# Rotary embedding in a fused decoder trunk: the swap of 32-row halves by ScalarE copies instead of DMAs inside the chip

## The reference

```python
def _rope(t, positions):
    ...
    t1, t2 = tf[..., : d // 2], tf[..., d // 2:]
    out = jnp.concatenate([t1 * cos - t2 * sin, t2 * cos + t1 * sin], axis=-1)

def _diff_attention_mixer(proj_tok, positions, lam_params, subln_g, layer_idx):
    q, k, v = jnp.split(proj_tok, 3, axis=-1)
    q = _rope(q.reshape(b, s, DIFF_HEADS, 2, DIFF_HEAD_DIM), positions)
    k = _rope(k.reshape(b, s, DIFF_HEADS, 2, DIFF_HEAD_DIM), positions)
    ...
    o = _diff_attention(q, k, v, lam)
    o = _rms_norm(o, subln_g) * (1.0 - lambda_init)
```

## Time and profile before

| | us |
|---|---|
| median of 3 runs | 978.41 |
| the three runs | 976.68, 978.41, 983.6 |
| profiled execution, first to last instruction (span) | 976.1 |
| PE busy | 951.2 |
| DVE busy | 636.7 |
| ACT busy | 469.7 |

### The profile page before, as it was taken

One profiled execution on the slowest core, in us unless ns is written; L12 is line 12 of the kernel. 1 busy time (PEld: TensorE's weight loads), 2 busy tenths in 40 slices (PEclk: granted clock), 3 DMA queues, 4 the chain that ended last, 5 costly groups with the idle time before them and its releaser, 6 DMA issues.

```text
span 976.1 us, 14093 instructions
## 1 busy us (share of the span) xinstructions
PE 951.2 (97%) x5161; PEld 819.9 (84%) x5161; DVE 636.7 (65%) x894; ACT 469.7 (48%) x708; POOL 1.2 (0%) x9
## 2 busy tenths in 40 slices
PE   6999999999999999999999999999999999999995
PEld 5788888888888888888888888888888888888884
DVE  5776656666666666655685465467877878777555
ACT  5756544444444443444464455446445364454441
POOL 0000000000000000000000000000000000000000
PEclk9999999999999999999999999999999999999998
DMA  9665465566666555656567645565565555746552
GB/s 317 222 230 182 136 210 173 184 203 193 194 191 191 186 186 192 210 186 202 166 230 202 189 141 195 169 204 158 176 190 152 177 167 155 198 151 203 198 177 86
DMA packets 149689, 182.30 MB, mean 187 GB/s; under 512 B 8016, under 2 KB 118928, under 8 KB 148880
## 3 DMA queue, kind: packets, MB, share of 16 engines
q1 hardware_dynamic: 148704, 177.25, 57.7%
q10 hardware_dynamic: 944, 4.49, 1.3%
HBM read 176.48 MB, written 2.10 MB: 183 GB/s over the span
## 4 chain that ended last, share of the span: by engine, by line
PE 71%; DVE 14%; DMA 5%; issue 4%; ACT 3%; SPq 2%; DVEq 0%; ACTq 0%
PE psum L340 27%; PE psum L341 13%; PE psum L369 9%; PE psum L368 9%; PE psum L367 9%; DVE lo_ring L794 5%; DMA layer_area<-layer_area 5%; SPq L277 2%; ACT layer_area L758 2%; PE psum L384 1%; DVE layer_area L801 1%; ACT hi_ring L588 1%; DVE psum L1088 1%; DVE layer_area L1065 1%; DVE columns L1092 1%
## 5 line engine op out<-in xcount | busy, mean ns | idle before, releaser
L340 PE MATMUL psum<-hT_split,hi_ring 128*128 128x512 f32 x1600 | 560.1, 396 | 0.0
L794 DVE TENSOR_TENSOR lo_ring<-raw_ring,hi_ring 128x1024 fp32r<-128x1024 f32 x320 | 386.3, 1223 | 240.5 <-ACT hi_ring L588 237.6
L588 ACT ACTIVATE hi_ring<-raw_ring 128x1024 fp32r<-128x1024 f32 x320 | 337.5, 1062 | 403.4 <-PE psum L341 262.1
L341 PE MATMUL psum<-hT_split,lo_ring 128*128 128x256 f32 x1600 | 445.3, 278 | 0.0
L340 PEld LDWEIGHTS psum<-hT_split,hi_ring 128*128 128x128 f32 x1600 | 300.6, 188 | 68.3
L341 PEld LDWEIGHTS psum<-hT_split,lo_ring 128*128 128x128 f32 x1600 | 301.3, 188 | 0.3
L367 PE MATMUL psum<-hi_ring,branchT_split 128*128 128x512 f32 x256 | 100.0, 391 | 0.0
L369 PE MATMUL psum<-hi_ring,branchT_split 128*128 128x512 f32 x256 | 99.7, 390 | 0.0
L368 PE MATMUL psum<-lo_ring,branchT_split 128*128 128x512 f32 x256 | 99.7, 390 | 0.0
L368 PEld LDWEIGHTS psum<-lo_ring,branchT_split 128*128 128x128 f32 x256 | 48.1, 188 | 10.0
L367 PEld LDWEIGHTS psum<-hi_ring,branchT_split 128*128 128x128 f32 x256 | 48.1, 188 | 9.9
(11 more groups left out here) (159 smaller groups left out, 650.7 us busy)
## 6 DMA issues: line engine op xcount, KB each, us to landing
raw_ring<-in_w_in_dram SPq DMA_DIRECT2D x224, 512.0 KB, 4.4
raw_ring<-in_w_out_dram SPq DMA_DIRECT2D x64, 512.0 KB, 4.8
raw_ring<-in_w_kv_mem_dram SPq DMA_DIRECT2D x32, 512.0 KB, 5.3
layer_area<-layer_area SPq DMA_DIRECT2D x48, 64.0 KB, 4.0
stage_area<-in_mem_dram SPq DMA_DIRECT2D x4, 512.0 KB, 7.5
x_residual<-in_x_dram SPq DMA_DIRECT2D x1, 2048.0 KB, 10.9
x_residual<-in_x_dram ACTq DMA_DIRECT2D x1, 2048.0 KB, 8.6
layer_area<-in_post_norm_dram ACTq DMA_DIRECT2D x2, 1024.0 KB, 6.2
```

The costliest lines, as they stand in the source:

```text
L340: mm(o, hi[:, k, P * c:P * (c + 1)], X[:, kt, :], start=kt == 0, stop=False)
L341: last = mm(o[:, SEQ:], lo[:, k, P * c:P * (c + 1)], X[:, kt, 0:SEQ], start=False, stop=kt == KT - 1)
L588: run(whi[:, slot, :], raw[:, slot, :], ACT.Copy).then_inc(hi_ready, 1)
L794: V_.tensor_tensor(wlo[:, slot, :], raw[:, slot, :], whi[:, slot, :].bitcast(f32), SUB)\
```

## The change

The four DMAs per swap become four ScalarE copies (`ACT.Copy`) of 32 x 512 numbers each, from one group of 32 partitions to its neighbour. The wait for the combine moves with them to ACT: it stands right behind `take_small` of the queries' group and of the keys' group. The semaphore `rot_loaded`, counted by 16, becomes `rot_copied`, counted by 1. SyncE's queue keeps the weights' loads alone, in the same order. DVE's program is the same but for the semaphore.

```diff
         with sp.Fori(0, PAIRS) as p:
             for g, col in enumerate((0, TOK_WIDTH, GATE_COL)):
                 column_group(p * (3 * B_UNITS) + (U_PAIR + B_UNITS * g), w_in[1], p * BCOLS + col)
-                if g == 0 and not first:
-                    swap_halves(p * 3 + (G_PAIR - 2), kT, krot)
-            swap_halves(p * 3 + G_PAIR, qT, qrot)
...
+        def swap_halves(G, src, dst):
+
+            act.wait_ge(bank_free, G + 1)
+            for b in range(4):
+                o = 32 * (b ^ 1)
+                run(dst[32 * b:32 * b + 32, :], src[o:o + 32, :], ACT.Copy).then_inc(rot_copied, 1)
+
         def pair(p, s, first=False):
             G, u = p * 3 + G_PAIR, p * (3 * B_UNITS) + U_PAIR
             column_group(G, u, s, at={} if first else {2: lambda: exps(p - 1)})
+            swap_halves(G, qT, qrot)
             column_group(G + 1, u + B_UNITS, 1 - s,
                          at={} if first else {2: lambda: take_weights(p - 1), 3: lambda: take_values(p - 1)})
+            swap_halves(G + 1, kT, krot)
             column_group(G + 2, u + 2 * B_UNITS, s)
             tanh_of(G + 2, val1, tanh1)
...
-        def rope(st, loads, t, rot, dsts):
+        def rope(st, copies, t, rot, dsts):
 
-            dve.wait_ge(rot_loaded, loads)
+            dve.wait_ge(rot_copied, copies)
```

More of the change, by code:

```diff
@@ L182, in build @@
     x_loaded, rows_loaded, misc_loaded = sem("x_loaded"), sem("rows_loaded"), sem("misc_loaded")
-    gpost_loaded, rot_loaded, out_stored = sem("gpost_loaded"), sem("rot_loaded"), sem("out_stored")
+    gpost_loaded, rot_copied, out_stored = sem("gpost_loaded"), sem("rot_copied"), sem("out_stored")
     late_loaded = sem("positions_lambda_loaded")
@@ L270, in _ @@
             row_group(U_V + A_UNITS * g, w_in[1], 2 * TOK_WIDTH + ACOLS * g, in_order)
[L272 to L279, removed]
+        with sp.Fori(0, PAIRS) as p:
             for g, col in enumerate((0, TOK_WIDTH, GATE_COL)):
                 column_group(p * (3 * B_UNITS) + (U_PAIR + B_UNITS * g), w_in[1], p * BCOLS + col)
-                if g == 0 and not first:
-                    swap_halves(p * 3 + (G_PAIR - 2), kT, krot)
-            swap_halves(p * 3 + G_PAIR, qT, qrot)
-        pair(0, first=True)
-        with sp.Fori(1, PAIRS) as p:
-            pair(p)
         column_group(U_XG1, w_in[1], XGATE_COL)
-        swap_halves(G_PAIR + 3 * PAIRS - 2, kT, krot)
         column_group(U_XG1 + B_UNITS, w_in[1], XGATE_COL + BCOLS)
@@ L1117, in rope_keys @@
             def rope_keys():
-                rope(st, p * 128 + 128, kT, krot, [(slice(0, P), kT)])
+                rope(st, p * 8 + 8, kT, krot, [(slice(0, P), kT)])
             in_query, in_keys, in_gate = {}, {}, {2: rope_keys}
@@ L1122, in pair @@
                 in_gate = {0: lambda: out_norm(st, p - 1), 2: rope_keys, 3: lambda: out_take(st, p - 1, 1 - parity)}
-            in_keys[2] = lambda: rope(st, p * 128 + 64, qT, qrot,
+            in_keys[2] = lambda: rope(st, p * 8 + 4, qT, qrot,
                                       [(slice(64 * m, 64 * (m + 1)), q_of_map[m]) for m in range(2)])
```

## The result

| | before | after |
|---|---|---|
| median, us | 978.58 (6 runs, 976.68 to 983.6) | 985.42 (6 runs, 985.12 to 988.86) |
| span of the profiled execution, us | 976.1 | 986.4 |

The changed kernel is slower: ratio 1.0065, 95% interval 1.0036 to 1.0094. Forecast were 978.0 us and no change. The time lies within the range that was given (973 to 986) and within the 1% that the forecast called no change, but no change at all lies outside the interval: the small gain of 0.4 us that was forecast is a loss of 6.8.

A forecast was written before the change was run, and what follows sets the result against it. A loop through the swap, 39.87 us a pair, slightly longer than PE's 38.7, set the pace. Sections 18.69 + 12.46 + 5.56 + 3.07 = 39.78 us saved 0.4 us in all: span 975.7 plus 2.3, 978.0 us; range 973 to 986.

The forecast's parts named there:

- The loop through the swap, balanced against PE: Pair's loop over DVE, ACT and the swap, in four sections: 39.87 us before, against PE's own 38.7 us.
- What is late next: ACT's copy of the turned weights, behind q's copies: PE waits before the value products (L520), 1 to 1.3 us a pair.
- The cost of a block of copies: Four ACT copies spaced 0.54 us, plus 0.03 to see the combine: 2.19 us, where DMAs took 6.49 and 5.71.
- the prediction's own sign of being wrong: Wrong if PE waits nowhere, waits at the units, or the period moves over 0.5 us with copies of the duration taken.
- The rival without overlap: ACT copies don't overlap where the partition group changes: 0.64 us apart, 40.6 us a pair, 981.9 us; chance 0.28.
- The values behind the weights: PE sees the turned weights' copy 0.03 us later; its products with the values then take 1.26 us.
- How many pairs pay: Gain of 0.09 us a pair over four or five periods, 0.4 us; PE bounds the first pair.
- The upper rival: Copies cost 0.85 us each, ACT's block before the turned weights too long: loop 42.3 us, 990.4 us; chance 0.10.
- the lower one: Copies near 0.28 us relieve the swap: loop 37.7 us, under PE's 38.7, PE's idle time goes, 973.5 us; chance 0.12.

The follow-up runs named there:

- halves: Changed kernel with each 32 x 512 copy made as two of 32 x 256 on the same partitions; 991.56 us, ratio to before 1.0148.
- two copies: Changed kernel with each block made two 128 x 512 copies to two tiles, without the exchange of halves; 972.84 us, ratio to before 0.9951.
- q by DMAs: Against the changed kernel, q's halves are swapped by DMAs as before, k's stay ScalarE copies; 982.88 us, ratio to before 1.0021.
- q's copies later: Changed kernel with q's four copies moved behind the copy of the turned weights on ScalarE, k's unmoved; 971.57 us, ratio to before 0.9917.
- both later: Changed kernel with q's copies behind the turned weights' copy and k's behind the next q0 and q1 high parts; 972.16 us, ratio to before 0.9911.
- one copy: Changed kernel with each block made one 128 x 512 copy, without the exchange of halves; 972.51 us, ratio to before 0.9935.

## Why the prediction was wrong

- **The loop through the swap, balanced against PE:** right. The four sections close to 40.90 us in the changed kernel as they closed to 39.87 before, and two sections of four didn't change by more than 0.01 us. PE's own work was put at 38.7 us a pair; it is 38.39.
- **What is late next:** right. PE's waits before L539 and L528 went, and one before L520 (now L504), released by the copy of the turned weights, took their place, 1.97 us in the pair shown, where I gave 1 to 1.3. The sentence that PE waits only before two things was not quite right, though: the view of the earlier trace rows has a third wait of PE, before L520 for ACT's copy of the turned weights (L743), once, 0.5 us, behind the last pair. It is the one that grew.
- **The cost of a block of copies:** this is the term that failed. "I take 0.54 us, since the length along the free dimension is the same" took the duration from the right row (0.63 measured) and the overlap from a row in which the group of partitions doesn't change. Measured are 0.65 us a step. That is 0.11 us on each of eight copies, 0.9 us a pair; with the 0.2 of the next point 39.78 + 0.9 + 0.2 = 40.9 us, the pair shown. By the prediction's own sign of being wrong (a period that moves by more than 0.5 us with copies of the duration taken) it failed here: the copies had their 0.63 us, and the period grew by 1.0 in the pair shown. The rival without overlap had this mechanism and forecast 40.6 us; it had a chance of 0.28 and should have had more, since DVE's double row showed the same loss at a change of the group. The rule of the Trainium skill, "VectorE: DVE Perf Modes", section "Two Vector instructions with no wait between them", is about Vector instructions; the experiments with halves and with two copies show the same on ACT, with 0.32 us against 0.43 and 0.54 against 0.65.
- **The values behind the weights:** 0.2 us too little. PE began 0.14 us after the copy of the weights, and not 0.03, and its products after a stop took 1.36 us (763.73 to 765.09), and not 1.26. With it the combine-to-combine section is 12.46 + 0.44 + 0.2 = 13.1.
- **How many pairs pay:** I had "four or five periods" at 0.09 us and let PE alone bound the first. It doesn't: the first period grew from 38.39 to 39.73 us, with a wait of PE of 1.07 us. A block at 0.54 us a copy would be 0.44 us shorter, so by these numbers (an estimate) some 0.6 us of the wait would have stayed. The rival's 981.9 us was too low for this reason, for the 0.2 us of the values in each pair, and because nothing in the prediction has the two paces of the last section. An average over the five periods is the honest measure.
- **The range:** that 985.4 us lies within it is in part luck. The upper end stood for the missing overlap with some spread of the executions. By the two traces the change costs 4.9 us, and 5.5 of the 10.3 us between the profiled spans come from a loop that it doesn't touch.
- **The upper rival** (ACT's block in front of the weights decides) had the right place and a price of the copies that they don't have. The relief of the lower one is real, 971 to 973 us, but it takes another order and not cheaper copies: at the place of the change a block of 1.15 us is just hidden, one of 2.6 is not.

## What to carry to other kernels

When work moves from a queue to an engine that runs in order, price what stands behind it on that engine, and from which row it is needed: here the same 48 copies cost 7 us in front of one small copy that PE waits for, and win 8 us behind it. A step between instructions holds only for the form of access that its row has; where a group of partitions changes, count the full duration. Where a loop over engines and the busiest engine's own work are within 1 us of each other, two small delays decide the sign, so follow the loop section by section. And try the parts alone, but compare their sections and not only their times: what the other part does can change too, as the landing of the DMAs did here.

## What the runs showed that was not expected

PE has two paces. In long stretches of the same matmuls, with no wait and the same granted clock of 1.00, a pair (512 and 256 columns) takes 0.3467 us in one trace and 0.3533 in another, 1.9% more. From 158 to 198 us, in the convolution's loop, which the change doesn't touch, before:

```profile
158.00:198.00 40.00, 40.00 (x233) 34.99 (x232) 25.64 (x29) 17.32 (x19) 0.00 (x0) 1.00 0.59 184
```

and after:

```profile
158.00:198.00 40.00, 40.00 (x228) 34.72 (x227) 24.53 (x28) 17.21 (x19) 0.00 (x0) 1.00 0.59 175
```

233 matmuls against 228. The first matmuls behind this loop start at

```profile
384.13 0.59 PE L409 MATMUL psum<-stage_area,vm 128*128 128x256 f32 x2
```

before, and after at

```profile
389.52 0.38 PE L393 MATMUL psum<-stage_area,vm 128*128 128x256 f32 x1
```

5.4 us later, of which 0.3 were there at the loop's start: half of the difference between the two profiled spans. In both traces PE comes to this loop without idle time, from 16 transposes at the full clock. Of the eleven traces of this case the convolution's loop is at the slow pace in four: the changed kernel's two, the halves and q by DMAs. The traces at the fast pace include kernels whose program is the same up to there. Many of the times of one kernel fall into groups some 5 us apart (before, in the six runs beside the changed kernel: 976.68 to 978.74 and 983.28 to 983.6; q's copies later: 970.59 to 973.48 and one of 977.68; two copies: 971.44 to 973.21 and 977.21 to 977.86), and 5 us is what this loop at the slow pace costs. That the loop makes the groups is not shown, since each kernel but the changed one has a single trace; other runs of the kernel before also lie between the groups (980.19 to 981.6).

In the pairs the pace of the units behind the value products differs from pair to pair: 0.347, 0.353, 0.347, 0.347 and 0.353 us a pair of matmuls in one trace of the changed kernel, and 0.353, 0.347, 0.353, 0.353 and 0.347 in the other, which is the same program. The slow pace appears at this place only in kernels in which the value products come right behind the copy of the turned weights, most of them with a wait of PE. In the kernel before, with q's copies later, with both later, with one copy and with q by DMAs all five are at 0.347. What decides the pace wasn't found.
